# Routing by tile inside the output projection, indirect row traffic without empty slots, ten weight buffers and last sums on TensorE in a hybrid encoder step

## The chip, the cores and the metric

The kernel runs on one core of a Trainium2 chip. Its engines are TensorE (PE), VectorE (DVE), ScalarE (ACT), GpSimd (POOL) and the queue engine SyncE (SP); 16 DMA engines move data between HBM and the on-chip memory. The metric is the device time of one execution in microseconds, as the median of three runs.

## What is computed

One layer of a streaming encoder for 544 tokens (512 of a prompt, 32 of a sample), all in float32. The first half mixes along time (a state-space branch and a pooling branch), the second is a mixture of experts. Cut to what matters here:

```
merged = sigmoid(gate_s) * o_s + sigmoid(gate_p) * o_p     # 544 x 1024
x = x + merged @ w_out                                     # output projection
xn = rmsnorm(x, g_ffn)
lg = xn @ w_router_group                                   # 4 groups
grp = argmax(lg); wg = max(softmax(lg))
le_sel = (xn @ w_router_expert)[grp]                       # 8 experts of that group
top_v, top_i = top_k(le_sel, 2)
wk = softmax(top_v) * wg                                   # two weights a token
y = sum over the two chosen experts e:
        wk * ((silu(xn @ w_gate[e]) * (xn @ w_up[e])) @ w_down[e])
out = rmsnorm(x + y, g_final)
```

There are 32 experts; each has three weight matrices of 2 MB (1024x512, 1024x512, 512x1024), so 96 of them, 201 MB in all. 544 tokens with two experts each make 1088 rows of work.

## The kernel before

Each engine has its program written out by hand, and semaphores tie them together. On-chip memory is one tensor, `arena`, and `ps` is the accumulator memory of TensorE; so nearly every row of the profile reads `arena` or `ps`, and the line number tells what it is.

**First half (to about 317 us).** GpSimd fills a block with zeros and, in two loops (L447, L449), stores it 25 times to the HBM tensor `x_rows` and 9 times to `y_rows`, 512 KB each. SP loads tokens, `w_in` and the state-space parameters (L339 `ssm_c`, L342 `ssm_b`) in program order. TensorE projects (L1220), runs the state-space branch (L1247 is its first product, into groups of 32 rows of `ps`) and the gated merge; L490 on GpSimd writes the merged block that the output projection reads.

**Output projection and routing.** Tokens are in five tiles, four of 128 and one of 32 (`TT = 5`). For tile `i` TensorE runs 16 products 128x512 (L1366, two MATMUL records each, since a float32 product is two instructions), VectorE adds the residual (L1046), ScalarE squares (L629), VectorE finishes the norm and scales (L1054), TensorE transposes (L1377). Routing comes only after all five: logits of all tiles (L1385, 40 products with 36 columns), the choice on VectorE (L1062 to L1095), ranks within the experts (L1396 to L1399), row numbers (to L1129). Then:

```
            pool.wait_ge(rows_ready, 1)
            for i in range(TT):
                for k in range(2):
                    pool.indirect_dma_start(out=x_rows, ...)      # L495
            ...
            sp.wait_ge(scattered, 16 * 2 * TT)                    # L381
            for j in range(2):
                sp.dma_start(xg[j], x_rows[j * P:(j + 1) * P, :]) # L383
```

Each expert has a tile of 64 slots in `x_rows`; two experts make a pair of 128 rows, which SP reads back as one block (L383, L394), empty slots included. `x_rows` and `y_rows` have extra rows for experts with more than 64 tokens, and every engine has code for that case (`overflow`), which first reads a flag.

**Experts.** For expert `e` TensorE runs `gate_up` (L1417, 32 records), after every second expert it transposes the next pair of rows (`turn_x`, L1409), then `down` of the expert before (L1430, 16 records) and `turn_gate_up` (L1424). ScalarE copies out gate and up (L660), the turned rows (L655) and computes silu (L665). VectorE multiplies (L1146) and copies the result (L1150), GpSimd stores it to `y_rows` in two halves of 64 rows x 2 KB (L502). Weights go through eight buffers of 2 MB (`RING`, `NS = 8`), in order gate, up, down:

```
            for l in range(4): load(l)            # after the gated merge
            psum_waits(sp, "out4")
            for l in range(4, 7): load(l)
            psum_waits(sp, "lg"); load(7)
            ...                                   # the wait and the two loads above
            for l in range(NS, 3 * NE):           # each waits for the user of load l - NS
```

**End.** GpSimd waits for all stores, reads the overflow flag (L300) and gathers two rows a token (L521, ten indirect transfers). Per tile VectorE adds the two weighted rows to the residual in `x_tok` (L717, L1172), ScalarE squares (L691), VectorE normalizes (L1181), SP stores (L409).

Of the kernel before, what the change touches and what calls it, by code (L numbers as in the profile page):

```python
# [15 lines left out]
ALU = mybir.AluOpType  # L16
# [10 lines left out]
ROWS = [128, 128, 128, 128, 32]  # L27
KD = D // P
# [14 lines left out]
MAIN = NE * TILE  # L43
NROWS = -(-(MAIN + 2 * NT + TILE) // P) * P
ZEROED = NROWS // P + (NROWS - MAIN) // P
# [31 lines left out]
O_XN2T = O_SGS  # L77
# [9 lines left out]
O_XN2 = O_USQ  # L87
O_JUNK = O_XN2 + TT * D
O_ROUT = O_Z


RING = (0, SLOT, O_D, O_F, 2 * SLOT, O_CPOW, O_MT, O_XN2T)
# [15 lines left out]
for _m in range(8):  # L108
    TASKS += [(f"gb{_m}", "act"), (f"ga{_m}", "dve"), (f"po{_m}", "dve")]
TASKS += [("out0", "dve"), ("out1", "dve"), ("x2t0", "act"), ("out2", "dve"), ("x2t1", "act"),  # L110
          ("out3", "dve"), ("x2t2", "act"), ("out4", "dve"), ("x2t3", "act"), ("x2t4", "act"),
          ("lg", "dve"), ("rank", "dve")]
# [8 lines left out]
def encoder_step(nc, a, out):  # L121
    ctx = ExitStack()
    with ctx:
        arena = ctx.enter_context(nc.sbuf_tensor("arena", [P, END], F32))
        ps = ctx.enter_context(nc.psum_tensor("ps", [P, 8, 512], F32))

        x_rows = nc.dram_tensor("x_rows", (NROWS, D), F32).ap()
        y_rows = nc.dram_tensor("y_rows", (NROWS, D), F32).ap()
# [18 lines left out]
        prm = misc(M_PAR, 92)  # L147
# [3 lines left out]
        ss, rstd = misc(M_SS, TT), misc(M_SS + 8, TT)  # L151
        fin_cols = misc(M_FIN, 64)
        inv = misc(M_INV, 60).rearrange("p (g c) -> p g c", g=4)
        diag16 = misc(M_MASK, 16)
        ebase = misc(M_EB, 32)
# [26 lines left out]
        par_rows = at(O_PARROWS, 128, 92)  # L182
# [23 lines left out]
        xn2 = at(O_XN2, TT * D).rearrange("p (i d) -> p i d", i=TT)  # L206
        xn2_t = at(O_XN2T, KD * NT).rearrange("p (k t) -> p k t", k=KD)
        junk1 = at(O_JUNK, D)
        ring = [at(o, SLOT) for o in RING]
        xg = [at(O_XN2 + n * D, D) for n in range(2)]  # L210
        xg_t = [at(O_XN2 + (2 + n) * D, D).rearrange("p (k t) -> p k t", k=KD) for n in range(2)]
        gu_rows = [at(O_XN2 + 4 * D + n * F, F) for n in range(2)]
        silu = [at(O_JUNK + n * 4 * TILE, 4 * TILE).rearrange("p (k t) -> p k t", k=4) for n in range(2)]
        h = [at(O_JUNK + (2 + n) * 4 * TILE, 4 * TILE).rearrange("p (k t) -> p k t", k=4) for n in range(2)]


        place = [O_ROUT]

        def small(*shape):
            words = 1  # L220
            for s in shape:
                words *= s
            ap = at(place[0], words)
            place[0] += words
            assert place[0] <= O_WR
# [8 lines left out]
        logits = small(TT, 36)  # L234
        onehot = [small(TT, NE) for _ in range(2)]
        chosen = small(TT, NE)
        weight = small(TT, 2)
        rows_f = small(TT, 2)
        rows_i = small(TT, 2).bitcast(I32)
        ranks = small(TT, NE)  # L240
        s_a, s_b, s_c, s_d = (small(TT) for _ in range(4))
        g_hot, g_exp = small(TT, EG), small(TT, EG)
        le_sel, i_hot = small(TT, EI), [small(TT, EI) for _ in range(2)]
        i_tmp = small(TT, EI)
        le_mul = small(TT, EG, EI)
        prefer = small(EI)
        counts = small(NE)
        tab_f = small(2, EXTRA, NE)
        rank_mul = small(TT, NE)
        e_neg = small(TT)  # L250
        table = small(2 * NE * EXTRA + 8)[0:1].bitcast(I32)
        y_sb = [small(F) for _ in range(2)]
# [6 lines left out]
        consts, zero_ready, rows_zeroed = sem("consts"), sem("zero_ready"), sem("rows_zeroed")  # L259
        toep_zero, taps_ready, taps_out, toep_in = sem("toep_zero"), sem("taps_ready"), sem("taps_out"), sem("toep_in")  # L260
# [36 lines left out]

        def overflow(eng, body):

            any_extra = eng.value_load(table[0:1, 2 * NE * EXTRA:2 * NE * EXTRA + 1], min_val=0, max_val=1)  # L300
            count = eng.alloc_register()
            eng.reg_mov(count, 1)
            with eng.If(any_extra > 0):
# [1203 lines left out]
```

## Time and profile before

| | |
|---|---|
| median of 3 runs | 1004.82 us (1004.16 to 1005.38) |
| profiled execution, its own time | 1002.53 us |
| its span, first to last instruction | 1000.8 us |
| PE busy | 802.5 us, 80% |
| DVE, ACT, POOL busy | 238.3, 118.1, 145.8 us |
| data moved | 277.48 MB, mean 277 GB/s |
| granted TensorE clock, mean | 0.905 |

Busy time of an engine is the time in which it had an instruction under way; a share of the DMA engines is the mean over all 16. In the page's second part the span is cut into 40 slices of 25 us. The granted clock is given as a part of 2.4 GHz: 1.00 is 2.4 GHz, 0.50 is 1.2 GHz.

### The profile page before, as it was taken

Reading aid. Unit: us, or ns where it says so; the run is one execution under the profiler, and the core shown is the slowest. Engines: PE = TensorE matmul, PEld = TensorE weight load, DVE = VectorE, ACT = ScalarE, POOL = GpSimd, SP = SyncE. Lnnn points to the kernel's source line nnn. Section 1 sums busy time; section 2 is a strip of 40 time slices with the busy share of each in tenths; the row PEclk is TensorE's granted clock in tenths of the full one; section 3 lists DMA queues with packets and bytes.
Section 4 is the critical chain, followed back from the end, with each engine's and each line's share of the span. In section 5 each row is a group of like instructions: output and inputs, shape, how many; then the busy total and the mean of one; then the engine's idle time right before and its main releaser. Section 6 shows DMA issues by size and latency. Waiting matters only on the chain. (4 is left out here: it accounts for less than half of the span.)

```text
span 1000.8 us, 9327 instructions
## 1 busy us (share of the span) xinstructions
PE 802.5 (80%) x3738; PEld 458.8 (46%) x3739; DVE 238.3 (24%) x618; ACT 118.1 (12%) x204; POOL 145.8 (15%) x282
## 2 busy tenths in 40 slices
PE   3899999999998998707978878797878779787800
PEld 2688888788885443703323333233333333233300
DVE  4739969100111122240000000000000000000036
ACT  4110120210000112001101010010101011010011
POOL 6300008810332000030000000000000000000040
PEclk9999999999998998558989898999999899889955
DMA  9996024070103503644999999999999999999561
GB/s 341 399 332 197 17 84 119 17 271 19 75 1 139 218 1 118 239 178 186 369 428 425 429 428 428 425 430 428 426 426 428 429 428 425 426 427 431 223 210 68
DMA packets 47644, 277.48 MB, mean 277 GB/s; under 512 B 12185, under 2 KB 13029, under 8 KB 35314
## 3 DMA queue, kind: packets, MB, share of 16 engines
q1 hardware_dynamic: 35388, 238.67, 58.3%
q0 software_dynamic: 11568, 36.58, 9.7%
q10 hardware_dynamic: 646, 1.64, 0.5%
q8 instruction: 30, 0.49, 0.2%
q14 instruction: 12, 0.10, 0.0%
HBM read 243.62 MB, written 33.26 MB: 277 GB/s over the span
## 5 line engine op out<-in xcount | busy, mean ns | idle before, releaser
L1417 PE MATMUL ps<-arena 128*64 128x512 f32 x1024 | 258.0, 661 | 85.6 <-DMA arena<-in_w_exp_up 84.5
L1220 PE MATMUL ps<-arena 128*128 128x272 f32 x1024 | 240.2, 396 | 0.0
L1220 PEld LDWEIGHTS ps<-arena 128*128 128x128 f32 x1024 | 196.1, 192 | 40.7
L1417 PEld LDWEIGHTS ps<-arena 128*64 128x64 f32 x1024 | 90.1, 151 | 231.4 <-issue 229.5
L1150 DVE COPY arena<-ps 128x512 f32<-128x512 f32 x32 | 22.1, 692 | 434.8 <-PE ps L1430 434.8
L1430 PE MATMUL ps<-arena 128*64 128x512 f32 x512 | 116.5, 595 | 1.1 <-DVE arena L1146 1.1
L502 POOL DMA_DIRECT2D y_rows<-arena x64 | 33.2, 523 | 472.5 <-DVE arena L1150 471.7
L708 DVE TENSOR_TENSOR arena<-arena 128x256 f32<-128x256 f32 (+14 forms) x231 | 78.1, 338 | 24.2 <-DMA arena<-in_ssm_b_im 16.4
L1366 PE MATMUL ps<-arena 128*128 128x512 f32 (+1 forms) x160 | 72.5, 614 | 3.0 <-POOL arena L490 3.0
L1430 PEld LDWEIGHTS ps<-arena 128*64 128x64 f32 x512 | 38.1, 137 | 64.3 <-issue 61.2
L660 ACT ACTIVATE arena<-ps 128x512 f32<-128x512 f32 x32 | 19.1, 597 | 330.2 <-PE ps L1417 330.2
L1366 PEld LDWEIGHTS ps<-arena 128*128 128x128 f32 (+1 forms) x160 | 28.6, 181 | 44.3 <-issue 44.3
L1409 PE MATMUL ps<-arena 128*128 128x128 f32 x128 | 19.3, 296 | 26.1 <-DMA arena<-x_rows 26.1
L1409 PEld LDWEIGHTS ps<-arena 128*128 128x128 f32 x128 | 16.1, 195 | 38.3 <-issue 38.3
L1424 PEld LDWEIGHTS ps<-arena 128*128 128x128 f32 x128 | 17.9, 209 | 26.7 <-issue 25.2
L573 ACT ACTIVATE arena<-ps 128x544 f32<-128x544 f32 x20 | 12.5, 624 | 140.4 <-PE ps L1220 140.4
L495 POOL DMA_INDIRECT x_rows<-arena x10 | 9.6, 962 | 121.4 <-DVE arena L1129 118.7
L1034 DVE TENSOR_TENSOR arena<-ps,arena 128x544 f32<-128x544 f32 x8 | 5.8, 725 | 88.8 <-PE ps L1220 88.8
L665 ACT ACTIVATE arena<-ps 128x256 f32<-128x256 f32 x32 | 12.3, 383 | 105.7 <-PE ps L1424 105.7
L1424 PE MATMUL ps<-arena 128*128 128x128 f32 x128 | 23.9, 310 | 0.7 <-ACT arena L660 0.7
L487 POOL TENSOR_TENSOR arena<-arena 128x544 f32<-128x544 f32 x8 | 10.7, 1338 | 90.4 <-DVE arena L1034 90.4
L1146 DVE TENSOR_TENSOR arena<-ps,arena 128x256 f32<-128x256 f32 x32 | 13.6, 424 | 39.5 <-ACT arena L665 39.4
(194 smaller groups left out, 456.0 us busy)
## 6 DMA issues: line engine op xcount, KB each, us to landing
arena<-in_w_exp_gate SPq DMA_DIRECT2D x32, 2048.0 KB, 29.0
arena<-in_w_exp_up SPq DMA_DIRECT2D x32, 2048.0 KB, 19.5
arena<-in_w_exp_down SPq DMA_DIRECT2D x32, 2048.0 KB, 24.6
x_rows<-arena POOLq DMA_DIRECT2D x25, 512.0 KB, 15.3
arena<-in_w_in SPq DMA_DIRECT2D x6, 2048.0 KB, 12.3
arena<-x_rows SPq DMA_DIRECT2D x16, 512.0 KB, 19.2
y_rows<-arena POOLq DMA_DIRECT2D x64, 128.0 KB, 6.9
y_rows<-arena POOLq DMA_DIRECT2D x9, 512.0 KB, 26.1
```

The costliest lines, as they stand in the source:

```text
L502: pool.dma_start(y_rows[e * TILE:(e + 1) * TILE, half * F:(half + 1) * F], y_sb[e % 2][half * TILE:(half + 1) * TILE]).then_inc(y_stored[e ...
L573: emptying(act.activation(halves(dst), pair(NUM[name])[:, :, 0:HALF], func))
L660: act.activation(gu_rows[par], ps[:, 2 + par, :], ACT.Copy).then_inc(gu_copied, 1)
L708: step(dve.tensor_tensor(out_, x0, x1, op))
L1146: dve.tensor_tensor(h[par], src[:, :, TILE:2 * TILE], silu[par], ALU.mult).then_inc(h_ready, 1)
L1150: dve.tensor_copy(y_sb[par], ps[:, 6 + par, :]).then_inc(y_ready, 1)
L1220: last = pe.matmul(dst[:, hh, 0:HALF], w[:, k, m * P:(m + 1) * P], rhs[:, k, hh * HALF:(hh + 1) * HALF], start=(k == 0), stop=(k == kk - 1))
L1366: last = pe.matmul(dst[:r, n, :], m_t[:, k, i * P:i * P + r], wn[:, k, :], start=(k == 0), stop=(k == 7))
L1409: last = pe.transpose(*turned)
L1417: last = pe.matmul(ps[n * TILE:(n + 1) * TILE, 2 + par, :], x_t[:, k, :], w[:, k, :], start=(k == 0), stop=(k == KD - 1))
L1424: last = pe.transpose(ps[:, 4 + par, k * P:(k + 1) * P], blocks[:, k, :], ident)
L1430: last = pe.matmul(ps[half * TILE:(half + 1) * TILE, 6 + par, :], h[par][:, k, :], w_down[:, k, half * F:(half + 1) * F], start=(k == 0), ...
```

## The change

Seven things are done at once.

1. `x_rows` is gone. The residual tiles are stored once, unnormalized, as `x2_rows` (544 rows), and each pair of experts gathers its 128 slots from it with one indirect transfer on GpSimd's queue; slots with no token have a row number out of bounds. `y_rows` becomes `y_parts`, where each half row of a result goes to its token's place (again indirect, out of bounds where empty). The 34 stores of zeros become one small one.
2. The output projection takes the tile of 32 rows first (`OUT_ORDER = (4, 0, 1, 2, 3)`), in four groups of 32 rows of `ps` and 256 columns each. The other tiles' products are cut in eight parts, and the routing of the tile before is put between them.
3. The slot table (which token sits in which slot) comes from products of one-hot rows (`slot_ids`, `slot_values`), summed over tiles.
4. The norm is not applied to the rows: `g_ffn` goes into the router's weights and into the copy of the turned rows (now on VectorE), the reciprocal root into ScalarE's copy of gate and up, the token's weight into the copy of the result.
5. Ten weight buffers; seven loads are issued after the merge, three after the projection.
6. At the end SP loads the two half results and the residual of a tile, TensorE sums the three with an identity, ScalarE squares from `ps`, VectorE scales from `ps`.
7. `g_ffn` is loaded as one more small parameter at the start; overflow is kept, by its own table.

The core of the diff:

```diff
+OUT_ORDER = (4, 0, 1, 2, 3)
-RING = (0, SLOT, O_D, O_F, 2 * SLOT, O_CPOW, O_MT, O_XN2T)
+RING = (0, SLOT, O_D, O_F, O_SGS, O_USQ, O_UT, 2 * SLOT, O_CPOW, O_XNT)
+EARLY = 7
...
@@ SP @@
-            for l in range(4):
+            sp.wait_ge(hist_out, 32)
+            for l in range(EARLY):
                 load(l)
-            psum_waits(sp, "out4")
-            for l in range(4, 7):
+            sp.wait_ge(out_done, 2 * TT)
+            for l in range(EARLY, NS):
                 load(l)
-            psum_waits(sp, "lg")
-            load(7)
-            sp.wait_ge(scattered, 16 * 2 * TT)
-            for j in range(2):
-                sp.dma_start(xg[j], x_rows[j * P:(j + 1) * P, :]).then_inc(xg_in[j], 16)
             for l in range(NS, 3 * NE):
...
-                if l % 6 == 4 and l // 6 + 1 < NP:
-                    sp.dma_start(xg[j % 2], x_rows[j * P:(j + 1) * P, :]).then_inc(xg_in[j % 2], 16)
+            sp.wait_ge(down_done, NE - 3)
+            sp.dma_start(ring[6]..., x2_rows[0:SEQ]...).then_inc(x2_back, 16)
...
+            sp.wait_ge(y_all, 1)
+            for i in range(TT):
+                sp.dma_start(y_end[i][:ROWS[i]], src).then_inc(y_back[i], 16)
@@ GpSimd @@
-            with pool.Fori(0, NROWS // P) as n:
-                pool.dma_start(x_rows[bass.ds(n * P, P), :], zeros).then_inc(rows_zeroed, 16)
-            with pool.Fori(MAIN // P, NROWS // P) as n:
-                pool.dma_start(y_rows[bass.ds(n * P, P), :], zeros).then_inc(rows_zeroed, 16)
...
+            for n, i in enumerate(OUT_ORDER):
+                pool.wait_ge(x2_ready, 2 * n + 2)
+                pool.dma_start(x2_rows[i * P:i * P + ROWS[i]], x_tok[:ROWS[i], i, :]).then_inc(x2_stored, 16)
+            def gather(j):
+                pool.indirect_dma_start(out=xg[j % 2], in_=x2_rows, ... x_row[:, j:j + 1] ...,
+                    bounds_check=NT - 1, oob_is_err=False).then_inc(xg_in[j % 2], 16)
             pool.wait_ge(rows_ready, 1)
+            for j in range(2):
+                gather(j)
             for e in range(NE):
+                if e % 2 == 0 and 2 <= e // 2 + 1 < NP:
+                    pool.wait_ge(xt_done, e // 2)
+                    gather(e // 2 + 1)
                 pool.wait_ge(y_ready, e + 1)
-                for half in range(2):
-                    pool.dma_start(y_rows[...], y_sb[e % 2][half * TILE:(half + 1) * TILE])
+                pool.indirect_dma_start(out=y_parts, ... y_row[:, e:e + 1] ..., in_=y_sb[e % 2],
+                    bounds_check=4 * NT - 1, oob_is_err=False).then_inc(y_stored[e % 2], 16)
@@ VectorE @@
+            for n in range(1, TT):
+                residual(n, 0)
+                slots(n - 1)
+                values(n - 1)
+                residual(n, 1)
+                norm(n)
+                take_ids(n - 1)
+                if n + 1 < TT:
+                    take_values(n - 1)
+                choose(n)
+            slots(TT - 1)
+            take_ids(TT - 1)
+            ts(unused, ids, 0.0, ALU.is_equal, skip_row, ALU.mult)
+            stt(y_row, ids, half_less_1, unused, ALU.add, ALU.add)
...
@@ TensorE @@
+            def out_part(n, part):
+                i, half = OUT_ORDER[n], part // 4
+                for k in (2 * (part % 4), 2 * (part % 4) + 1):
+                    last = pe.matmul(ps[:, 2 * (n % 2) + half, :], m_t[:, k, i * P:(i + 1) * P], ...)
...
+            for n in range(1, TT):
+                out_part(n, 0)
+                turn_x2(n - 1, 0)
+                turn_x2(n - 1, 1)
+                out_part(n, 1)
+                if n >= 2:
+                    slot_values(n - 2)
+                out_part(n, 2)
+                logits(n - 1, 0)
+                logits(n - 1, 1)
+                for part in (3, 4, 5):
+                    out_part(n, part)
+                ranks(n - 1)
+                out_part(n, 6)
+                if n == TT - 1:
+                    turn_x2(n, 0)
+                out_part(n, 7)
+                slot_ids(n - 1)
...
+            for i in range(TT):
+                pe.wait_ge(y_back[i], 16)
+                for half in range(2):
+                    for n, part in enumerate(parts):   # residual, first, second result
+                        last = pe.matmul(ps[:r, 2 * (i % 4) + half, :], ident[0:r, 0:r], part, start=(n == 0), stop=(n == 2))
```

The order of TensorE's instructions from the first output product on. `x32` counts products as the program has them (a float32 product is two records in the trace, a transpose one). Before:

```order
L1366 MATMUL ps<-arena 128x512 x32
L1377 MATMUL ps<-arena 128x128 x8
L1366 MATMUL ps<-arena 128x512 x16
L1377 MATMUL ps<-arena 128x128 x8
L1366 MATMUL ps<-arena 128x512 x16
L1377 MATMUL ps<-arena 128x128 x8
L1366 MATMUL ps<-arena 32x512 x16
L1377 MATMUL ps<-arena 128x128 x8
L1377 MATMUL ps<-arena 128x32 x8
L1385 MATMUL ps<-arena 128x36 x32
L1385 MATMUL ps<-arena 32x36 x8
```

Now, for the small tile (L1554) and the first full tile (L1495 are its products; L1507 transposes, L1517 logits, L1526 ranks, L1535 slot table, all of the small tile):

```order
L1554 MATMUL ps<-arena 32x256 x32
L1495 MATMUL ps<-arena 128x512 x2
L1507 MATMUL ps<-arena 128x32 x8
L1495 MATMUL ps<-arena 128x512 x4
L1517 MATMUL ps<-arena 32x36 x8
L1495 MATMUL ps<-arena 128x512 x6
L1526 MATMUL ps<-arena 32x32
L1495 MATMUL ps<-arena 128x512 x4
L1535 MATMUL ps<-arena 128x32 x2
L1495 MATMUL ps<-arena 128x512 x2
L1507 MATMUL ps<-arena 128x128 x8
```

The logits, which stood behind all 80 output products, stand between those of the next tile. At the end of the last full tile the same engine has, up to the first expert (L1591 turns the first pair, L1599 is `gate_up`):

```order
L1507 MATMUL ps<-arena 128x128 x4
L1495 MATMUL ps<-arena 128x512 x2
L1535 MATMUL ps<-arena 128x32 x2
L1517 MATMUL ps<-arena 128x36 x4
L1507 MATMUL ps<-arena 128x128 x4
L1517 MATMUL ps<-arena 128x36 x4
L1526 MATMUL ps<-arena 128x32
L1528 MATMUL ps<-arena 128x32
L1545 MATMUL ps<-arena 128x64 x2
L1535 MATMUL ps<-arena 128x32 x2
```

Behind the last output product (second row) there are 4 transposes and 18 small products (the last two follow these rows), where 40 logits products and 20 of ranks stood before. GpSimd's queue in the expert stage, for two pairs:

```order
L524 DMA arena<-x_rows,arena 128x1024 x2
L538 DMA y_parts<-arena 2176x512 x2
L524 DMA arena<-x_rows,arena 128x1024
L538 DMA y_parts<-arena 2176x512 x2
```

The gather of a pair (L524) stands between the stores of results (L538), where before only the stores stood (and SP's queue had the reads).

## Rows read from the trace of the kernel before

**Rows 1.** The page's second part: busy tenths of the DMA engines in 40 slices.

```profile
DMA  9996024070103503644999999999999999999561
```

**Rows 2.** Stages: length, busy us (and count) of each engine, clock, DMA share, GB/s.

```profile
391.00:457.00 66.00, 27.57 (x148) 25.66 (x148) 22.45 (x99) 5.37 (x9) 9.62 (x10) 0.53 0.56 219
465.00:935.00 470.00, 385.15 (x1686) 152.45 (x1684) 33.92 (x61) 47.03 (x78) 31.14 (x60) 0.93 1.00 423
```

**Rows 3.** The start: timeline (start, length, what), a stage, a group of transfers.

```profile
12.35 8.09 SPq L339 DMA_DIRECT2D arena<-in_ssm_c_im  x4
39.49 0.82 PE L1233 MATMUL ps<-arena 128*128 128x128 f32 x4 [3.74 <-DMA arena<-in_ssm_c_im]
40.00:45.00 5.00, 5.00 (x17) 3.91 (x16) 4.14 (x24) 0.00 (x0) 0.29 (x1) 0.67 1.05 411
x_rows<-arena POOLq DMA_DIRECT2D x25, 512.0 KB, 15.3
```

**Rows 4.** Timeline of the output projection.

```profile
317.02 13.15 PE L1366 MATMUL ps<-arena 128*128 128x512 f32 x23 [3.01 <-POOL arena L490]
363.09 13.90 PE L1366 MATMUL ps<-arena 128*128 128x512 f32 x32
376.83 1.04 PE L1377 MATMUL ps<-arena 128*128 128x128 f32 x8
391.75 1.21 DVE L1046 TENSOR_TENSOR arena<-ps,arena 32x1024 f32<-32x1024 f32 x1 [9.47 <-PE ps L1366]
```

**Rows 5.** Timeline: products into four groups of 32 rows.

```profile
122.43 2.03 PE L1247 MATMUL ps<-arena 128*32 128x128 f32 x64
```

**Rows 6.** Timeline from the projection's end to the first expert.

```profile
398.61 14.94 PE L1385 MATMUL ps<-arena 128*128 128x36 f32 x80 [0.52 <-ACT arena L638]
417.34 0.20 DVE L717 SCALAR_TENSOR_TENSOR arena<-arena 128x40 f32<-128x40 f32 x1
435.37 1.13 POOL L495 DMA_INDIRECT x_rows<-arena  x1 [118.69 <-DVE arena L1129]
453.69 1.94 PE L1409 MATMUL ps<-arena 128*128 128x128 f32 x8 [26.06 <-DMA arena<-x_rows]
456.74 8.53 PE L1417 MATMUL ps<-arena 128*64 128x512 f32 x32 [1.11 <-ACT arena L655]
465.32 0.33 SPq L369 DMA_DIRECT2D arena<-in_w_exp_down  x1
```

**Rows 7.** Expert stage: transfers (KB each, us from issue to landing), two timeline rows.

```profile
arena<-x_rows SPq DMA_DIRECT2D x16, 512.0 KB, 19.2
y_rows<-arena POOLq DMA_DIRECT2D x64, 128.0 KB, 6.9
arena<-y_rows,arena POOLq DMA_INDIRECT x10, 5.3
536.52 7.09 PE L1417 MATMUL ps<-arena 128*64 128x512 f32 x32 [1.94 <-DMA arena<-in_w_exp_up]
543.41 3.63 PE L1430 MATMUL ps<-arena 128*64 128x512 f32 x16
```

**Rows 8.** Timeline of the last experts and of the end.

```profile
920.12 8.78 PE L1417 MATMUL ps<-arena 128*64 128x512 f32 x32 [4.09 <-DMA arena<-in_w_exp_up]
935.39 7.09 PE L1417 MATMUL ps<-arena 128*64 128x512 f32 x32 [2.37 <-DMA arena<-in_w_exp_up]
952.40 1.03 POOL L502 DMA_DIRECT2D y_rows<-arena  x2 [4.37 <-DVE arena L1150]
957.71 1.03 POOL L521 DMA_INDIRECT arena<-y_rows,arena  x1 [4.27 <-issue]
964.34 1.29 DVE L717 SCALAR_TENSOR_TENSOR arena<-arena 128x1024 f32<-128x1024 f32 x1 [12.23 <-DMA arena<-y_rows,arena]
994.17 1.05 ACT L691 ACTIVATE arena<-arena 32x1024 f32<-32x1024 f32 x1 [4.88 <-DVE arena L1172]
996.80 1.27 DVE L1181 SCALAR_TENSOR_TENSOR arena<-arena 32x1024 f32<-32x1024 f32 x1
```

More of the change, by code:

```diff
@@ L303, in overflow @@
             with eng.If(any_extra > 0):
+                if first is not None:
+                    first()
                 with eng.Fori(0, NE * EXTRA) as i:
@@ L1103, in _ @@
-            step(dve.memset(ranks[:, 4], 0.0))
-            step(dve.tensor_copy(ranks[:32, 4], rk[:32, 0, 4 * NE:5 * NE]))
-            empty(dve.tensor_copy(counts, rk[:, 1, 0:NE]), read=True)
-            full = (P, TT, NE)
-            beyond, first = small(NE), [small(NE), small(NE)]
-            ts(beyond, counts, -float(TILE), ALU.add, 0.0, ALU.max)
-            step(dve.memset(first[0][:, 0:1], 0.0))
-            step(dve.tensor_copy(first[0][:, 1:NE], beyond[:, 0:NE - 1]))
-            shift, n = 1, 0
@@ new lines, in _, with x_out @@
+            by_pair = y_row.rearrange("p (j two) -> p j two", two=2)
+            for half in range(2):
+                part = slice(64 * half, 64 * half + 64)
+                last = dve.tensor_scalar(x_row[part], by_pair[part, :, half], 2, None, ALU.logical_shift_right)
+            last.then_inc(rows_ready, 1)
+            take_values(TT - 2)
+            values(TT - 1)
+            take_values(TT - 1)
+            dve.sem_inc(slot_w_ready, 1)
+            def x_out(par, turned, t=P):
+                dve.wait_ge(xt_done, turned)
+                src = ps[:, 0:2, :].rearrange("p h (k t) -> p (h k) t", k=4)
+                dve.tensor_tensor(xg_t[par][:, :, 0:t], src[:, :, 0:t], g_x.unsqueeze(2).to_broadcast((P, KD, t)),
+                                  ALU.mult).then_inc(xt_ready, 1)
@@ new lines, in logits, with ranks @@
+            def logits(n, half):
+                r = ROWS[OUT_ORDER[n]]
+                pe.wait_ge(x2t_ready, 2 * n + half + 1)
+                if n:
+                    pe.wait_ge(val_taken, min(n, TT - 2))
+                for k in range(4 * half, 4 * half + 4):
+                    last = pe.matmul(ps[:r, 6, 0:36], x2_t[n % 2][:, k, 0:r], w_r[:, k, :], start=(k == 0), stop=(k == KD - 1))
+                if half:
+                    last.then_inc(lg_done, 1)
+            def ranks(n):
+                r = ROWS[OUT_ORDER[n]]
+                pe.wait_ge(chosen_ready, n + 1)
+                if n:
+                    pe.wait_ge(before_ready, n)
+                last = pe.matmul(ps[:r, 7, P:P + NE], tri[:r, :r], chosen[n % 2][:r], start=True, stop=(n == 0))
+                if n:
+                    last = pe.matmul(ps[:r, 7, P:P + NE], ones[:, :r], before, start=False, stop=True)
+                last.then_inc(rank_done, 1)
@@ L1404, in turn_x @@
+            logits(TT - 1, 0)
+            turn_x2(TT - 1, 1)
+            logits(TT - 1, 1)
+            ranks(TT - 1)
+            slot_values(TT - 2)
+            slot_ids(TT - 1)
+            slot_values(TT - 1)
             def turn_x(par, rows):
```

635 lines of the change are left out of this document (374 added, 261 removed).

## The prediction

> **What bounds the kernel now.** I read the busy shares in slices first, then the stages, then the timeline at the seams, then the transfers. The slices show DMA at 9 from the 20th slice to the 37th, idle stretches before and 5 6 1 behind [rows 1]. Three stretches follow. To 391.7 us TensorE runs almost without a gap. From 391.7 to 456.7 us it is busy 27.6 of 66 us at a clock of 0.53, and DMA at 56%: a serial chain of routing [rows 2]. From 465 to 935 us all DMA engines are busy (1.00, 423 GB/s) while TensorE has 385 of 470 us: the experts are bound by the transfer of weights. From there about 66 us are a serial end.
>
> So whatever lets the stream of weights begin earlier, or takes bytes out of it, counts in full; TensorE, VectorE and ScalarE in that stage do not.
>
> **Start: -5 us.** The zero stores (25 of 512 KB in one group, 34 in all, 17.8 MB) share the DMA engines with everything from 12 us on. TensorE waits 3.7 us for `ssm_c`, whose issue began at 12.35 us and took 8.1 us, and the clock then is 0.67 for 5 us, which costs (1 - 0.67) x 5 = 1.6 us [rows 3]. Issued by 20.4 us and needed at 35.7 us, it should be there without those stores: 5 us; bounds 0 and 5.4. One more small load at the start may cost some tenths. What follows on TensorE has no gap of note, and VectorE, which waits longer for `ssm_b`, gains at least as much, so the 5 us arrive at the first output product: 312 instead of 317 us.
>
> **Projection: -1.5 us.** It takes 317.0 to 391.7, 74.7 us, of which a tile is 32 records in 13.9 us, 0.43 each, and its transposes 1.04 us [rows 4]. The small tile costs as much as a full one. Now its 64 records of 256 columns go into four groups of 32 rows; the nearest row has 64 records of 128 columns into such groups in 2.03 us [rows 5], so twice that, 4 us. Four full tiles stay 55 us. Between them stand 32 transposes (4 us), four times the logits, 16 records of 0.187 us at the low clock [rows 6], half that at full clock, so 6 us, and about 10 to 12 records of slot products a tile, 4 us together. 4 + 55 + 14 = 73 us, end at 385. Work on VectorE for a tile is some 40 short operations of 0.20 us and a few long ones, 11 us, under the 17 us that a tile takes on TensorE; the tightest place is `choose`, 16 dependent operations of 0.20 + 0.03 us (3.7 us) between logits and ranks, under three parts of 1.7 us. If that cover is missing, each tile pays the excess, 1 to 3 us.
>
> **Chain after the projection: -43.5 us.** Before it is 65.0 us (391.7 to 456.7): 14.9 us of logits, VectorE's choice, ranks, the row numbers at 435.4, ten scatters, reading back, first product at 453.7 [rows 6]. Now, for the last tile alone: half a residual, transposes, copy and logits, 4.2 us; `choose` 3.7; ranks, one-hot rows, `slot_ids` and five operations for the row numbers 4.3 (products at the low clock); gather issued 0.3 later and landed in 5.3, as the ten gathers at the end [rows 7]; turning 1.9, and VectorE's copy of 128x1024 from `ps`, as L1046 1.2, with gaps 3.7. Sum 21.5 us. The stores of the residual tiles on the same queue are issued 5 us earlier at least. `gate_up` of expert 0 starts at 406.5 and ends after 8.5 us at 415, where SP issued at 465.3 [rows 6]. So the stream restarts 50 us earlier.
>
> **Bytes in the stream: -10 and -10 us.** Ten buffers instead of eight: two loads of 2.1 MB leave the stage, at 423 GB/s 9.9 us. Their transfer lies in front, where DMA is idle from some 350 to 385 us. The rows: before, 14 reads of 512 KB and 64 stores of 128 KB, 15.7 MB. 1088 of 2048 slots are filled, so at best 8.3 MB stay: -17.4 us. At worst nothing comes off, if a skipped row takes its engine's time or the filled ones lie unevenly over the 16 engines, since a load ends with its slowest engine. No row shows which; I take -10, a little over half.
>
> The Trainium skill, DMA: Bandwidth & Descriptors, section The descriptor swizzle, spreads partitions over engines in fours: of a half of 64, partitions 0 to 31 give each of eight engines four rows and the next ones go to the first engines again. By it an expert with 36 tokens or more loads the first engine as 64 would, and one with 32 or fewer half as much; for counts spread around 34 about half of the 17.4 us would come off, 9 us, and the sum would stay at 931. No run here shows it.
>
> **End: -4 us.** From the last store's issue (952.4) to the end (1000.8) it is 48.4 us. Store and flag take 5.3 us to 957.7 [rows 8]; that stays. Then SP loads 1 MB for the first tile: between 2.5 us (at 423 GB/s) and 6.6 us (957.7 to 964.3, two gathers of 512 KB); I take 4.7. TensorE: 30 products, 60 records of 512 columns at 0.43 us, 25.8 us; it comes cold, and a cold start cost 8.78 - 7.09 = 1.7 us in rows 8, here 2. VectorE needs only some 3 us a tile for what stays with it, so TensorE's 5.2 us a tile are the bound. From the last square to the end it was 6.6 us (994.2 to 1000.8). 5.3 + 4.7 + 27.8 + 6.6 = 44.4 us. VectorE's (998.1 - 964.3) / 5 = 6.8 us a tile are exchanged for almost as many on TensorE. Reading `x2_rows` back (2.2 MB) lies behind the last weights, under 16 us of TensorE's work.
>
> **What is newly in the expert stage.** The copy of the turned rows goes to VectorE (busy 34 of 470 us), beside `down` of 3.6 us: nothing. GpSimd's queue now has the gather between the stores. It can only be issued when the store before it is, so a pair of experts has a loop: result copied and store issued 2.4 us, landing L, turning 1.2, `down`, `turn_gate_up`, `gate_up`, `down` 3.6 + 0.8 + 7.1 + 3.6 [rows 7], together 18.7 + L. The stream gives 2 x 15.4 = 30.8 us a pair (442 us for 28.7 experts). So L may be 12 us; stores on that queue landed in 6.9 us in this stage, so it is hidden.
>
> **Sum.** Of the span 1000.8: -5 - 1.5 - 43.5 - 9.9 - 10 - 4 = -74, so 926.8 us. The profiled execution's own time is 1.7 us above its span and the median 2.3 us above that time: 930.8, I say 931 us.
>
> **Rivals.**
> - *Skipped slots save nothing:* 931 + 10 = 941 us. For it: SP's loads use all engines alike and wait for the slowest; against: bytes not moved should not cost. 0.18.
> - *The sums run at the low clock:* idle for 10 us, TensorE starts cold, and 60 records at 0.86 us are 51.6 instead of 27.8 us: 955 us. For it: 0.53 in the routing stage; against: that work was small products with waits, and dense ones of 512 columns regained the full clock in 1.7 us of loss [rows 8]. 0.08.
> - *The routing does not hide in the projection:* `choose` and the slot rows arrive late, 2 to 3 us a tile, and the last tile's chain is 5 us longer: +15, 946 us. For it: over 60 operations and 6 hand-overs a tile; against: the slack above. 0.10.
> - *The gather sets the pace (slower than before):* if L is beyond 12 us, each us costs 15 us. At 19.2 us, the row of the same bytes read on SP's queue [rows 7], it is 7.2 x 15 = 108 us: 1039 us. It decides against the change from L = 17. Against it: those reads stood in line behind weights on SP's queue, 6.9 and 5.3 us are this queue's. 0.03. The DMA page of the Trainium skill (Queues, rings and completion order) has each engine take turns between queues, which is what 6.9 beside 19.2 shows.
> - *All cancels out:* 0.01.
>
> **How the numbers follow.** The forecast has 0.60; its own range is 919 to 942, from the bounds of start (0 to 5.4), padding (0 to -17.4), tail load (2 us) and 4 us for the chain. With the two near rivals inside, 80% lie in 917 to 948. Measurement tells 0.2% from nothing. Faster: all but the gather's case, 0.96; same 0.01; slower 0.03.
>
> **What would show it.** Right: no zero stores and no wait for `ssm_c`; first output product at 312; small tile 4 us; rows for the first gather at 397; first `gate_up` at 406 or 407; DMA at 1.00 from 415 to about 862 with fewer MB; GpSimd's gathers landing in 7 to 9 us and never ending TensorE's wait; sums of 0.43 us a record. Wrong: a TensorE wait between parts of the projection, DMA share below 1.00 in the expert stage, TensorE waiting for the gathered rows, a clock of 0.50 in the last 40 us.

## The result, and the profile after

The changed kernel takes 988.6 us (median of four runs, 985.8 to 991.7) against 1004.5 us before (also of four runs; the table above has the first three): ratio 0.984, 95% interval 0.981 to 0.988. It is faster, as forecast, but by 16 us and not by 74, and it lies far outside the range of 917 to 948 us. The profiled execution took 986.8 us, of which the span is 985.2. In each of experiments 4 and 6 one execution, of 1850 and of 1663 us, is left out of the median.

The seams first. In the rows of the changed kernel the name `x_rows` stands for `x2_rows`, since the profile leaves numbers out of names. Timeline of the changed kernel from the last product of the output projection to the first expert (L1495 is the projection, L1526 the ranks, L1545 the slot values, L524 the gather, L1591 the turning of the rows, L1599 gate and up; rows of TensorE, then GpSimd, then SP):

```profile
312.91 5.18 PE L1554 MATMUL ps<-arena 128*32 128x256 f32 x64 [2.87 <-issue]
...
386.44 1.88 PE L1495 MATMUL ps<-arena 128*128 128x512 f32 x4
...
395.98 0.64 PE L1526 MATMUL ps<-arena 128*128 128x32 f32 x2 [4.16 <-DVE arena L1163]
...
410.40 1.97 PE L1591 MATMUL ps<-arena 128*128 128x128 f32 x8 [7.15 <-DMA arena<-x_rows,arena]
...
413.76 9.39 PE L1599 MATMUL ps<-arena 128*64 128x512 f32 x32 [1.12 <-DVE arena L1239]
```
```profile
401.55 1.09 POOL L524 DMA_INDIRECT arena<-x_rows,arena  x1 [11.67 <-DMA x_rows<-arena]
```
```profile
423.19 0.33 SPq L387 DMA_DIRECT2D arena<-in_w_exp_up  x1
```

The reader is to see that the front half kept most of its promise: the first output product stands at 312.9 us instead of 317.0 [rows 4], and SP issues the first load that had to wait for an expert at 423.2 us instead of 465.3 [rows 6]. 42 us are won here, where 50 were forecast. The tail is as forecast too. Timeline from the last expert's store to the end (L538 the store, L424 the reading back of the experts' rows, L1677 the sums):

```profile
941.02 0.98 POOL L538 DMA_INDIRECT y_parts<-arena  x1 [4.69 <-DVE arena L1271]
945.96 2.50 SPq L424 DMA_DIRECT2D arena<-y_parts  x5
950.78 28.16 PE L1677 MATMUL ps<-arena 128*128 128x512 f32 x60 [11.42 <-DMA arena<-y_parts]
```

985.2 - 941.0 = 44.2 us, against 48.4 before. Between 423 and 941 us lies what went wrong. The gate and up product of expert 0 ends at 423.2, the last store is issued at 941.0: 518 us, where it was 487 before (465.3 to 952.4), though by the forecast 20 us of transfers had been taken out of the stage. The page's groups of the costliest instructions show where (busy us, mean ns | idle us before, releaser):

```profile
L1591 PE MATMUL ps<-arena 128*128 128x128 f32 x128 | 30.7, 417 | 115.9 <-DMA arena<-x_rows,arena 115.9
```

115.9 us of idle time in 15 waits for the gathered rows, one of 7.15 us at the front and 14 in the stage. Stage 500 to 880 us (columns as in rows 2) of the changed kernel, and two groups of transfers of the whole run, the stores and the gathers (median us from issue to landing):

```profile
500.00:880.00 380.00, 294.38 (x1258) 109.40 (x1256) 40.52 (x57) 23.92 (x45) 34.33 (x34) 0.85 0.93 384
```
```profile
y_parts<-arena POOLq DMA_INDIRECT x32, 7.9
arena<-x_rows,arena POOLq DMA_INDIRECT x16, 12.4
```

The DMA engines are busy 0.93 of the time and move 384 GB/s; before they were saturated at 423 [rows 2]. So neither the transfers nor TensorE (busy 294 of 380 us) is the bound: a chain of waits is. One turn of it, first on TensorE, then on GpSimd (L1612 down, L1606 turning of gate and up):

```profile
495.84 1.97 PE L1591 MATMUL ps<-arena 128*128 128x128 f32 x8 [7.68 <-DMA arena<-x_rows,arena]
497.74 4.94 PE L1612 MATMUL ps<-arena 128*64 128x512 f32 x16
502.61 0.75 PE L1606 MATMUL ps<-arena 128*128 128x128 f32 x4
503.29 7.09 PE L1599 MATMUL ps<-arena 128*64 128x512 f32 x32
510.20 3.60 PE L1612 MATMUL ps<-arena 128*64 128x512 f32 x16
...
529.31 1.97 PE L1591 MATMUL ps<-arena 128*128 128x128 f32 x8 [7.81 <-DMA arena<-x_rows,arena]
```
```profile
515.46 0.99 POOL L538 DMA_INDIRECT y_parts<-arena  x1 [10.12 <-DVE arena L1271]
516.75 1.04 POOL L524 DMA_INDIRECT arena<-x_rows,arena  x1 [0.30 <-issue]
```

From the turning at 495.84 to the issue of the next gather at 516.75 it is 20.9 us, from there to the next turning at 529.31 another 12.6: 33.5 us for a pair of experts. The loop is run 14 times, from the turning at 431.70 to the one at 903.77 us, 33.7 us each on average:

```profile
431.70 1.16 PE L1591 MATMUL ps<-arena 128*128 128x128 f32 x8
...
903.77 1.97 PE L1591 MATMUL ps<-arena 128*128 128x128 f32 x8 [7.48 <-DMA arena<-x_rows,arena]
```

The gather stands behind the store of the expert before in GpSimd's program, that store behind `down`, and `down` behind the turning that waits for the last gather.

### The profile page after: what moved, and what is told of

It is laid out like the page before. It is cut to its first block and busy times, and to the rows that moved or that the text cites. A ratio compares the mean times of both kernels' runs of the same rounds, so it can differ in the third digit from the quotient of the medians.

```text
span 985.2 us, 9611 instructions
## 1 busy us (share of the span) xinstructions
PE 819.2 (83%) x3850; PEld 454.0 (46%) x3851; DVE 261.4 (27%) x743; ACT 119.9 (12%) x230; POOL 128.2 (13%) x224
## 3 DMA queue, kind: packets, MB, share of 16 engines
q0 software_dynamic: 6672, 12.86, 3.5%
## 5 line engine op out<-in xcount | busy, mean ns | idle before, releaser
L1599 PE MATMUL ps<-arena 128*64 128x512 f32 x1024 | 229.1, 600 | 1.1 <-DVE arena L1239 1.1
L1349 PEld LDWEIGHTS ps<-arena 128*128 128x128 f32 x1024 | 195.6, 192 | 40.4
L1612 PE MATMUL ps<-arena 128*64 128x512 f32 x512 | 141.0, 702 | 1.3 <-DVE arena L1267 1.3
L1599 PEld LDWEIGHTS ps<-arena 128*64 128x64 f32 x1024 | 71.2, 138 | 134.7 <-issue 129.7
L1591 PE MATMUL ps<-arena 128*128 128x128 f32 x128 | 30.7, 417 | 115.9 <-DMA arena<-x_rows,arena 115.9
L538 POOL DMA_INDIRECT y_parts<-arena x32 | 32.0, 999 | 487.2 <-DVE arena L1271 487.2
L1591 PEld LDWEIGHTS ps<-arena 128*128 128x128 f32 x128 | 24.5, 218 | 129.3 <-DMA arena<-x_rows,arena 128.4
L1239 DVE TENSOR_TENSOR arena<-ps,arena 128x1024 f32<-128x1024 f32 x16 | 19.6, 1225 | 238.6 <-PE ps L1591 238.6
L1612 PEld LDWEIGHTS ps<-arena 128*64 128x64 f32 x512 | 41.3, 163 | 89.2 <-issue 87.5
L1271 DVE TENSOR_SCALAR arena<-ps,arena 128x512 f32<-128x512 f32 x32 | 24.0, 751 | 217.4 <-PE ps L1612 217.4
L769 DVE TENSOR_TENSOR arena<-arena 128x256 f32<-128x256 f32 (+10 forms) x223 | 75.5, 339 | 11.4 <-ACT arena L681 3.9
L1495 PE MATMUL ps<-arena 128*128 128x512 f32 x128 | 59.6, 603 | 0.0
L724 ACT ACTIVATE arena<-ps,arena 128x512 f32<-128x512 f32 x32 | 22.0, 687 | 231.1 <-PE ps L1599 231.1
L1677 PE MATMUL ps<-arena 128*128 128x512 f32 (+1 forms) x60 | 28.2, 629 | 11.4 <-DMA arena<-y_parts 11.4
L1495 PEld LDWEIGHTS ps<-arena 128*128 128x128 f32 x128 | 22.7, 190 | 21.7 <-issue 21.5
L1606 PEld LDWEIGHTS ps<-arena 128*128 128x128 f32 x128 | 17.9, 209 | 26.9 <-issue 25.1
L1606 PE MATMUL ps<-arena 128*128 128x128 f32 x128 | 23.9, 309 | 0.9 <-ACT arena L724 0.9
## 6 DMA issues: line engine op xcount, KB each, us to landing
arena<-in_w_glu_a SPq DMA_DIRECT2D x1, 2048.0 KB, 10.6
```

Source lines behind the costliest of these rows:

```text
L538: pool.indirect_dma_start(out=y_parts, out_offset=bass.IndirectOffsetOnAxis(ap=y_row[:, e:e + 1], axis=0), in_=y_sb[e % 2], in_offset=None ...
L724: act.activation(gu_rows[par], ps[:, 2 + par, :], ACT.Copy, scale=scale).then_inc(gu_copied, 1)
L769: step(dve.tensor_tensor(out_, x0, x1, op))
L1239: dve.tensor_tensor(xg_t[par][:, :, 0:t], src[:, :, 0:t], g_x.unsqueeze(2).to_broadcast((P, KD, t)), ALU.mult).then_inc(xt_ready, 1)
L1271: dve.tensor_scalar(y_sb[par], ps[:, 6 + par, :], scale, None, ALU.mult).then_inc(y_ready, 1)
L1349: last = pe.matmul(dst[:, hh, 0:HALF], w[:, k, m * P:(m + 1) * P], rhs[:, k, hh * HALF:(hh + 1) * HALF], start=(k == 0), stop=(k == kk - 1))
```

## The experiments

Theory A: this loop through the gather sets the pace of the stage. Rival B: the transfers are the bound in either form, and the wait for the gather only stands where the wait for weights stood. The first four kernels tell these apart and price the empty slots; the next ones price the ring, the front and what makes the landing long. The diffs are against the changed kernel, if not said otherwise.

**1. Gather one pair sooner.**

```
-                if e % 2 == 0 and 2 <= e // 2 + 1 < NP:
-                    pool.wait_ge(xt_done, e // 2)
-                    gather(e // 2 + 1)
+                if e % 2 == 0 and e // 2 + 2 < NP:
+                    pool.wait_ge(xt_done, e // 2 + 1)
+                    gather(e // 2 + 2)
```

> The gather of pair j+2 is issued once the rows of pair j are turned, one pair (two experts) sooner than in the changed kernel; nothing else differs. Theory A (the gather sets the pace: 33.4 us for a pair, of which 12.4 to 12.8 us are its landing, against 30.8 us for the weights of a pair at the 427 GB/s of before): the 15 waits of 7.7 us of the turning of rows go, the gate and up projections wait for weights again, the stage from first to last expert falls from 517.8 us to 465 to 480, and the time from 988.6 to 935 to 950. Rival B (the wait for the gather only stands where the wait for weights would stand, since the transfers are the bound either way): 983 to 989 us, with the waits moved to the gate and up projections.

Measured 937.0 us (936.5 to 937.4, ratio 0.933 [0.931, 0.935]): theory A, and 51.7 us faster than the changed kernel. Two groups of its page and a stretch of its stage:

```profile
L1599 PE MATMUL ps<-arena 128*64 128x512 f32 x1024 | 255.0, 655 | 69.9 <-DMA arena<-in_w_exp_up 68.7
L1591 PE MATMUL ps<-arena 128*128 128x128 f32 x128 | 19.3, 296 | 7.0 <-DMA arena<-x_rows,arena 7.0
```
```profile
500.00:600.00 100.00, 83.14 (x370) 33.09 (x368) 11.96 (x16) 7.12 (x13) 9.13 (x9) 0.93 1.01 427
```

The wait for the rows is left once (7.0 us, at the front), the wait for weights is back, and DMA is at 1.01 and 427 GB/s. The gather still lands in 12.4 us; it is merely no longer waited for. Rival B is out.

**2. Gather ahead of the store.** GpSimd issues the same gather just before the store of the odd expert and not just behind it.

> The gather is issued just before the store of the expert's rows, not just behind it. Theory A: it starts 1.3 us sooner, which is worth 15 x 1.3 = 20 us by itself, 969 us. If the store ahead of it in the queue is also why it lands in 12.4 us and not in 8.5 (as the first did), 15 x 5 us are to be had, down to the weights' own pace: 940 us. Rival B (transfers are the bound either way): 985 to 989 us.

Measured 939.9 us (0.937 [0.934, 0.939]), theory A's second figure.

```profile
arena<-x_rows,arena POOLq DMA_INDIRECT x16, 10.6
```
```profile
L1591 PE MATMUL ps<-arena 128*128 128x128 f32 x128 | 30.7, 417 | 72.2 <-DMA arena<-x_rows,arena 72.2
```

The gather is issued 1.3 us sooner and lands in 10.6 instead of 12.4 us, so the store ahead of it in the queue costs it 1.8 us; the stores, now behind it, land in 8.9 instead of 7.9 us. That takes 3.1 us off the loop, which is now about 30.5 us (two turnings start at 640.72 and 671.22). It is also the stream's own pace: 426 GB/s are held from 500 to 800 us, and TensorE still waits for rows, 72 us, but not for weights. The loop and the stream have come to the same length, and some 3 us off each loop were 49 us in all.

**3. A plain read instead of the indirect one.** The chosen rows are replaced by 128 neighbouring ones.

```
+                pool.dma_start(xg[j % 2], x2_rows[j % 4 * P:(j % 4 + 1) * P, :]).then_inc(xg_in[j % 2], 16)
```

> Each indirect gather becomes a plain read of 128 whole rows that lie one behind the other, on the same queue at the same place; this leaves out the choice of the rows, so the outputs are not the reference's. 544 KB or so become 128 rows, 512 KB, a pair, 8 or so more per cent on this read than with the empty slots left out. If the indirect form makes the landing long, it falls to about 8 us and the time to 945 to 960 us. If the weights' stream beside it and the store ahead of it make it long, the landing stays at 11 to 13 us and the time at 980 to 992 us.

Measured 992.2 us, the read landing in 13.2 us:

```profile
arena<-x_rows POOLq DMA_DIRECT2D x16, 512.0 KB, 13.2
```

The landing and the time both lie a hair above the second case's bounds (13 and 992 us) and far from the first's. An indirect gather of all 128 rows (experiment 4) also lands in 13.2 us, so the indirect form is not what makes it long.

**4. Empty slots moved after all.** Experiment 1 with `SKIP = 4 * NT + 4` and 132 more rows in `x2_rows` and `y_parts`; a store also waits for the one before, since both hit the spare rows.

> The first experiment's kernel (gathers one pair sooner), with real rows behind each expert's empty slots: the gathers and the stores move all 64 slots of an expert and not 21 to 43, which is 960 more rows of 4 KB in and of 2 KB out, 5.9 MB. The prediction's step (10 us, bounds 0 and 17.4): this run is 10 us slower than the first experiment, 14 us at 427 GB/s. Rival (skipped slots save nothing): the same time within 1 us.

Measured 947.1 us, 10.1 us more than experiment 1. The expectation misnamed the bytes: a slot's result is two rows of 2 KB, so 960 slots are 7.9 MB, 18.4 us at 427 GB/s, and the forecast's 10 us were set against that. So leaving slots out gives back about half of what its bytes are worth. The queue's own megabytes (packets, MB, share) are 21.26, of which 0.5 are zeros, against 12.86:

```profile
q0 software_dynamic: 6848, 21.26, 5.8%
```

The stores' extra wait is not in the 10.1 us: in the stage GpSimd waits only for VectorE's results and TensorE nearly only for weights (77.3 us). The steady part says the same: turnings there are 31.8 us apart (568.48 to 727.67, five pairs) where experiment 1 has 31.2 (566.15 to 722.04), 0.66 us for the 0.49 MB of a pair, which are worth 1.15. The gather landed in 13.2 us with all 128 rows and in 12.4 with the filled ones alone (1088 / 16 = 68 a pair on average): its length hardly depends on how many rows it moves. Both agree with the Trainium skill, DMA: Bandwidth & Descriptors, section The descriptor swizzle, by which rows 0 to 31 of a half already give every one of its engines four rows and the next go to the first engines again: the fullest engine has as many rows with 36 tokens as with 64. By that rule the prediction's estimate was 9 us; no run here shows the engines apart.

**5. Eight buffers.** Experiment 1 with `RING` two slots shorter and the last sums' tiles moved.

> The first experiment's kernel (gathers one pair sooner, 937.0 us) with eight weight buffers, as before the change, instead of ten; the last sums' tiles lie elsewhere for it. The prediction's step: two loads more stand in the stage that the transfers bound, 2 x 2.1 MB at 427 GB/s = 9.8 us, so 946.8 us. Rival (the depth of the ring does not matter, since the stream is steady and the two loads lie in front of it either way): 937 to 938 us.

Measured 941.0 us (0.938 [0.936, 0.940]), 4.0 us more than experiment 1, neither the 9.8 nor nothing. The timeline shows a second effect of the same edit:

```profile
404.58 1.97 PE L1591 MATMUL ps<-arena 128*128 128x128 f32 x8 [2.12 <-DMA arena<-x_rows,arena]
...
407.94 10.07 PE L1599 MATMUL ps<-arena 128*64 128x512 f32 x32 [1.12 <-DVE arena L1239]
```

There is one late load instead of three, and it has long landed by then. From the issue of the first gather to its turning it is 3.9 us instead of 8.9 in experiment 1, and the first gate and up ends at 418.0 instead of 421.95 us. So by an estimate two loads cost 4.0 + 3.9 = 8 us, and the ring's last two buffers hand half of their gain back at the front.

**6. Late loads held back.** Experiment 1, and SP waits for the first gather before the last three of the ten loads.

```
             sp.wait_ge(out_done, 2 * TT)
+            sp.wait_ge(xg_in[0], 16)
             for l in range(EARLY, NS):
```

> The first experiment's kernel, with the three loads of weights that are issued at the end of the projection held back until the first gather has landed; they are needed only some 25 us later. If their 6.3 MB beside it are why the first gather lands in 8.5 us, it lands in 5 to 6, and the first expert and all behind it come 3 us sooner: 934 us. Rival (the gather's own round trip is 8.5 us): no change, 937 us, or up to 1 us more if a later expert waits for the third load.

Measured 933.9 us, 3.1 us under experiment 1. These are only three runs, from 929.0 to 934.8 us, and the same kernel has 931.9 us further down, so the size is 3 to 5 us. The trace shows what is won at the front: the rows are turned from 405.4 instead of 409.3 us, and the first gate and up ends at 418.8 instead of 421.95 us, 3.1 us sooner as expected:

```profile
405.41 1.97 PE L1592 MATMUL ps<-arena 128*128 128x128 f32 x8 [2.34 <-DMA arena<-x_rows,arena]
```

**7 and 8. Smaller packets of weights.** In the changed kernel each partition's 16 KB are put together from four places (experiment 7) or from two (experiment 8).

```
-        experts = [....rearrange("e (p k) n -> e p (k n)", p=P) ...]
+        experts = [....rearrange("e (q p k) n -> e p q (k n)", q=4, p=P) ...]
```

> The changed kernel with each load of weights made of packets of 4 KB instead of 16 KB (a partition's row comes from four places); this leaves out the right order of the weights' rows, so the outputs are not the reference's. Bytes and work are the same. Theory C (each row of the gather stands in its DMA engine behind one packet of weights; a full engine has 8 rows; 16 KB at 427 / 16 = 26.7 GB/s take 0.61 us, 4 KB 0.15 us): the landing falls from 12.4 to about 9 us, and with it the pair from 33.4 us to the stream's own pace: 940 to 950 us, if the stream keeps its 427 GB/s. Rival (the gather's share of the bandwidth or its own latency sets 12.4 us): landing 12 to 13 us, time 985 to 992 us.

> As the run with packets of 4 KB, but with 8 KB; the outputs are not the reference's, since this leaves out the right order of the weights' rows. With packets of 16 KB the gather landed in 12.4 us, with 4 KB in 7.5 us: 0.41 us more for each KB. Theory C (each row of the gather waits in its engine behind a packet of weights): it lies on that line, 9.1 us, and the pair's loop through the gather is then 33.4 - 3.3 = 30.1 us, about the stream's own pace: 938 to 950 us. Rival (4 KB helped in another way, say since the stream fell to 410 GB/s and left room): landing 11 us or more with the stream at 427 GB/s, and 965 us or more.

Measured 955.0 and 943.8 us (0.952 and 0.941). The 8 KB run came out as expected; the 4 KB run lies 5 us above its range of 940 to 950, which held only if the stream kept 427 GB/s, and it fell to 409. The gather of the 4 KB run, then of the 8 KB run, each with its stage:

```profile
arena<-x_rows,arena POOLq DMA_INDIRECT x16, 7.5
```
```profile
500.00:880.00 380.00, 308.99 (x1328) 121.49 (x1326) 42.90 (x60) 24.99 (x47) 36.47 (x36) 0.91 1.03 409
```
```profile
arena<-x_rows,arena POOLq DMA_INDIRECT x16, 9.1
```
```profile
500.00:880.00 380.00, 322.95 (x1394) 121.59 (x1392) 44.09 (x62) 26.78 (x50) 37.59 (x38) 0.91 1.01 420
```

7.5, 9.1 and 12.4 us for 4, 8 and 16 KB lie on one line of 0.41 us a KB, with the same bytes, queues and work. So the length of the packets in the other queue sets how long a small gather takes. That its rows stand behind those packets is the reading of it, and no run shows that directly: an estimate of 8 rows an engine, each behind one piece of 16 KB at 427 / 16 = 26.7 GB/s, gives 0.3 us a KB, three quarters of the slope. The Trainium skill, DMA: Bandwidth & Descriptors, section Queues, rings and completion order, has each engine go round between queues, but drain a batch of some 9 to 17 pieces from one before it goes on; by it the gather as a whole would stand behind a batch of weights, and by an estimate the batch of a load in 16 KB pieces, 8 of them on an engine, would be 4.9 us. Which of the two it is stays open: both grow with the size, and no run here has the engines apart. The stream itself pays for small packets: 427 GB/s with 16 KB (experiment 1), 420 and 409 here, so 8 KB is the better of the two.

**9. Rows turned behind `down`.** In the changed kernel TensorE's `turn_x` moves from ahead of `down` and `turn_gate_up` to behind them.

> The changed kernel with its gathers where they are, but TensorE turns the gathered rows behind the down projection of the expert before and the turning of its gate and up rows, not ahead of them. Theory A (the loop of 33.4 us a pair through the gather sets the pace, and these 4.4 us of work stand behind the wait without need): they fill the wait, the loop falls by 3.6 + 0.75 us to about 29 us, below the stream's pace, and the time to 938 to 948 us. Rival B (what is waited for is only the order in which transfers share the bandwidth): 985 to 989 us.

Measured 958.4 us (0.954 [0.952, 0.956]): 30 us faster by order alone, but 10 us short of what was expected. A loop:

```profile
657.05 1.97 PE L1591 MATMUL ps<-arena 128*128 128x128 f32 x8 [4.88 <-DMA arena<-x_rows,arena]
660.41 8.65 PE L1599 MATMUL ps<-arena 128*64 128x512 f32 x32 [1.39 <-DVE arena L1239]
668.89 3.60 PE L1612 MATMUL ps<-arena 128*64 128x512 f32 x16
...
688.81 1.97 PE L1591 MATMUL ps<-arena 128*128 128x128 f32 x8 [4.51 <-DMA arena<-x_rows,arena]
```

It is 31.8 us and not 29: `down` and `turn_gate_up` (5.7 us with their slow start) left it, but VectorE's copy of the turned rows had been hidden beside `down` and now stands in the path with 1.4 us, the slow start after the idle time moved to gate and up, 8.65 instead of 7.09, and the gather lands in 13.1 us in this run, not in 12.4.

**10 to 12. A warm front.** Experiment 6 with products into a bank that is written anew later, in the gaps of TensorE's chain behind the projection: 8 + 5 + 6 of them, then 4 + 3 + 2, and experiment 6 once more beside the latter.

```
+            fill(4)
             ranks(TT - 1)
             slot_values(TT - 2)
             slot_ids(TT - 1)
+            fill(3)
             slot_values(TT - 1)
+            fill(2)
```

> The kernel with the late loads held back (934.4 us), with 19 products of 128x512 that nothing reads in three gaps of TensorE's chain behind the projection, 8 + 5 + 6, into a bank that is written anew later. Theory D (the lower clock in that chain is TensorE's idle time, and it costs on the path 3 to 4 us: turning 1.97 and not 1.16, first gate and up 9.3 to 10 and not 7.1, small products twice): 930 to 931 us. Rival (the clock comes back no sooner, or the fillers push the real ones back by as much): 934 to 937 us.

> As the run with fillers, with 4 + 3 + 2 products instead of 8 + 5 + 6. There each product counted twice, 0.43 us twice, so the fillers were longer than their gaps and pushed the chain back by 3.1 us, as much as the clock gave back; now they take 3.4, 2.6 and 1.7 us at full clock and end inside the gaps of 4.2, 2.9 and 2.3 us. Theory D: the first gate and up projection ends 3 us sooner than without fillers, 930 to 931 us. Rival (less work does not keep the clock): no change, 933 to 935 us.

> The kernel with the late loads held back once more, so that it stands beside the one with fillers on the same chip: 934 us, 2 to 3 us under the 937.0 us without the hold.

Measured 933.8 with the long fillers, 931.2 (929.1 to 932.0) with the short ones, 931.9 (930.7 to 934.9) without. First gate and up product with the long fillers, with the short ones, and without:

```profile
411.92 7.09 PE L1608 MATMUL ps<-arena 128*64 128x512 f32 x32 [1.24 <-DVE arena L1240]
```
```profile
408.02 7.09 PE L1608 MATMUL ps<-arena 128*64 128x512 f32 x32 [1.25 <-DVE arena L1240]
```
```profile
408.64 8.41 PE L1600 MATMUL ps<-arena 128*64 128x512 f32 x32 [1.12 <-DVE arena L1240]
```

With either the granted clock is 1.00 (2.4 GHz) from 400 to 425 us, against 0.70 and 0.77 without, and the product takes 7.1 instead of 8.4 to 10.1 us. The long ones push the chain back by as much. The expected 930 to 931 us were missed by the long ones. The short ones end the product 1.9 us sooner, but in the whole time 0.8 us of that is seen, inside the spread: it can't be told from nothing. The fastest kernels are thus experiment 1 with the late loads held back, at 932 to 934 us, with or without fillers.

## Why the prediction was right or wrong

**The step that failed** is *What is newly in the expert stage*: "So L may be 12 us; stores on that queue landed in 6.9 us in this stage, so it is hidden." The prediction saw the loop, wrote it as 18.7 + L against the stream's 30.8 us, and then took L from a transfer that is not of its kind. The runs showed 21.3 + 12.4 = 33.7 us in its place, 14 times, and about 50 us lost. Three things were off in the step.
- L was 12.4 us. The row of 6.9 us was a store of 128 KB, 64 rows of 2 KB [rows 7], where a gather spans 128 rows of 4 KB and has the 128 of a store just ahead of it. Experiments 2, 7 and 8 price what made it long: 1.8 us for the store ahead, and 0.41 us for each KB in the packets of weights. But by the prediction's own price this alone is (12.4 - 12) x 15 = 6 us. L took away the whole margin; the cost came from the next two.
- The 18.7 us were 20.9 in the loop shown and 21.3 on average (33.7 - 12.4). TensorE starts slowly after a wait of 8 us: turning took 1.97 instead of 1.16 us and `down` 4.2 to 5.8 instead of 3.6. The granted clock was 0.50 (1.2 GHz) from 495 to 498 us and 1.00 (2.4 GHz) again from 503 to 510. Without a wait, in experiment 1, the same two take 1.16 and 3.6 us: the wait feeds itself.
- The limit was not 30.8 us. That is about the stream's pace once the ring is empty (the turnings of experiment 1 are 31.2 us apart there), and the stage starts with ten loads in stock. The stage of experiment 1 took 468.3 us (421.95 to 890.24). In the changed kernel 8.6 us of the stage lie ahead of the first loop (423.15 to 431.70) and 37.3 behind the last (903.77 to 941.02), so for 14 loops there would be (468.3 - 8.6 - 37.3) / 14 = 30.2 us each. The loop began to cost from about L = 30.2 - 21.3 = 9 us, not from 12; experiment 8, with L = 9.1 and a stream of 420 GB/s, stands at 943.8 us. And (33.7 - 30.2) x 14 = 49 us is the loss.

Where the 50 us between the stages of the changed kernel and of experiment 1 went is seen on TensorE, which waits or works all the time. Groups of the changed kernel from 423 to 941 us, then of experiment 1 from 421.9 to 890.3 us:

```profile
L1599 PE MATMUL ps<-arena 128*64 128x512 f32 x994 | 220.3, 595 | 0.0
L1612 PE MATMUL ps<-arena 128*64 128x512 f32 x512 | 141.0, 702 | 1.3 <-DVE arena L1267 1.3
L1591 PE MATMUL ps<-arena 128*128 128x128 f32 x120 | 28.7, 416 | 108.8 <-DMA arena<-x_rows,arena 108.8
```
```profile
L1599 PE MATMUL ps<-arena 128*64 128x512 f32 x994 | 246.3, 652 | 68.7 <-DMA arena<-in_w_exp_up 68.7
L1612 PE MATMUL ps<-arena 128*64 128x512 f32 x512 | 116.4, 595 | 1.3 <-DVE arena L1267 1.3
L1591 PE MATMUL ps<-arena 128*128 128x128 f32 x120 | 17.4, 288 | 0.0
```

108.8 us of waiting against 68.7, `down` 141.0 against 116.4, turning 28.7 against 17.4, gate and up 220.3 against 246.3 (there the slow start falls on them): 40.1 + 24.6 + 11.3 - 26.0 = 50.0 us, and the stages are 517.9 - 468.3 = 49.6 us apart. The rival *The gather sets the pace* had this mechanism in the right place, at 0.03 and with a price of 15 us for each us over 12; its chance and its threshold were the error. It was argued against with 6.9 and 5.3 us of this queue beside 19.2 us on SP's, but the 6.9 us are of stores a quarter of the size. It did not come to L = 17, so the time stayed below that of before.

**What held.** With the gather out of the way (experiment 1) the time is 937 us; the range had 917 to 948.
- *Start:* 4.1 us of 5. No zero stores, no wait for `ssm_c`.
- *Projection, -1.5:* nothing. It takes 312.9 to 388.3 us, 75.4 instead of 74.7; the small tile took 5.2 and not 4 us, a full one with its routing 16.5 to 18.1. But TensorE waited for nobody between the parts: the rival *The routing does not hide* is out.
- *Chain, -43.5:* the first gate and up started at 413.8 and not at 406.5. 3.3 us are the projection's, 0.7 the chain's up to the gather's issue (401.55 and not 397.5), and 3.2 come behind it, where the gather lands in 8.5 us instead of 5.3, beside the three late loads (experiment 6 takes that back). Gate and up itself took 9.4 instead of 8.5 us.
- *Two loads fewer, -9.9:* 8 us (estimate of experiment 5).
- *Empty slots, -10:* 10.1 us (experiment 4), between bounds that were both wrong for it. The -10 was a choice between 0 and -17.4, so that it hit is partly luck; *Skipped slots save nothing* is out.
- *Stage:* the forecast's own end points, 415 and 882.4, are 467.4 us apart, experiment 1's 468.3.
- *Tail:* 44.2 us of 44.4, sums at 0.47 us a record; *The sums run at the low clock* is out.

So the sum was short by 8 us at the front, and by 50 for the loop. With the first alone, 939 us, the time would have stayed inside the range of 917 to 948 us; the range had no room for the second.

## What to carry to other kernels

A gather that is issued behind the results of one step and needed in the next closes a loop; write the loop down with everything in it, and let the margin stand against the landing beside a saturated stream, not against the nearest transfer in the list. When an edit moves a transfer into a queue of stores, ask first whether it can be issued one buffer sooner: here that was worth 52 us, while leaving out half of its rows took 0.8 us off its landing. And a threshold worked out from the steady pace and from engines that never wait is too generous: the ring starts full, and the wait makes the loop longer.

## What the runs showed of the hardware that was not expected

- A gather with about half of its 128 rows filled landed in 12.4 us, with all of them in 13.2, and a plain read of 128 rows in 13.2; with no weights beside it its rows were being turned 3.9 us after its issue (experiment 5). Its time is far more that of the traffic beside it than of its bytes.
- The size of the packets in a bulk stream is paid by the small transfers beside it: 16, 8 and 4 KB made 12.4, 9.1 and 7.5 us of the same gather, and the stores went from 7.9 to 6.7 and 6.1 us; the stream ran at 427, 420 and 409 GB/s.
- Nine spare products, 7.7 us of TensorE's time in the gaps, brought the granted clock from 400 to 425 us from 0.77 to 1.00 (experiments 12 and 11); in the whole time nothing clear of the spread came of it.
